# Two-block transformer kernel: order of the last two gate segments, form of the convolution norm, and placement of activation table loads

## What is computed

```python
def hybrid_layer(x, w_in, b_in, conv_w, conv_b, conv_ln_g, conv_ln_b, sinks, w_out, b_out, ln_g, ln_b):
    proj = jnp.einsum("bsd,de->bse", x, w_in) + b_in
    c_val, c_glu, c_gate, q, k, v, a_gate = jnp.split(proj, SPLIT_POINTS, axis=-1)
    y_conv = conformer_conv_branch(c_val, c_glu, conv_w, conv_b, conv_ln_g, conv_ln_b)
    y_conv = y_conv * jax.nn.silu(c_gate)
    y_attn = swa_sink_attention(q, k, v, sinks) * jax.nn.silu(a_gate)
    y = jnp.concatenate([y_conv, y_attn], axis=-1)
    y = jnp.einsum("bse,ed->bsd", y, w_out) + b_out
    return layer_norm(DEEPNORM_ALPHA * x + y, ln_g, ln_b)
```

## Time and profile before

| what | value |
|---|---|
| median of 3 runs (2601.18 to 2603.5) | 2602.79 us |
| the profiled execution's own time | 2602.43 us |
| its span, first to last instruction | 2600.6 us |
| PE busy | 2526.0 us, 97% of the span, 13143 matmuls |
| DVE busy | 1445.0 us, 56% |
| ACT busy | 1208.4 us, 46% |
| mean granted TensorE clock | 0.99 of full speed |

### The profile page before, as it was taken

The page is one execution under the profiler, slowest core; times in us unless marked ns, Lnnn a source line. Parts: engine busy times, 40 slices in busy tenths (PEclk is TensorE's granted clock), DMA queues, the critical chain, the costliest instruction groups (busy, mean ns, idle before and its releaser), DMA issues.

```text
span 2600.6 us, 34916 instructions
## 1 busy us (share of the span) xinstructions
PE 2526.0 (97%) x13143; PEld 2171.3 (83%) x13143; DVE 1445.0 (56%) x1937; ACT 1208.4 (46%) x1569; POOL 46.8 (2%) x58
## 2 busy tenths in 40 slices
PE   8999989999999999999999999999999999999786
PEld 8999978888888888888998888888888888887675
DVE  5555555545545445456755554545454545887755
ACT  5444545444444444445444544444444445556653
POOL 0000000000000000000220000000000001000000
PEclk9999999999999999999999999999999999999988
DMA  7555545666666665555545666666665657664433
GB/s 229 163 170 164 161 153 178 195 192 187 188 190 187 191 191 191 191 188 165 154 137 175 189 187 190 189 187 189 189 192 188 191 190 222 187 179 138 153 108 119
DMA packets 290789, 463.31 MB, mean 178 GB/s; under 512 B 17167, under 2 KB 115649, under 8 KB 290170
## 3 DMA queue, kind: packets, MB, share of 16 engines
q1 hardware_dynamic: 288384, 453.63, 57.6%
q0 software_dynamic: 1680, 8.11, 0.9%
q10 hardware_dynamic: 618, 0.09, 0.0%
HBM read 459.63 MB, written 2.14 MB: 178 GB/s over the span
## 4 chain that ended last, share of the span: by engine, by line
PE 94%; ACT 3%; DVE 2%; issue 1%; ACTq 0%; DVEq 0%
PE PG L246 72%; PE PG L224 12%; PE PG L235 4%; PE PS L767 1%; PE PS L706 1%; ACT ws L196 1%; PE PS L810 1%; PE PS L552 1%; PE PO L830 1%; DVE ws L202 1%; ACT ts L1578 0%; PE PS L768 0%; ACT ts L793 0%; PE PG L1142 0%; PE PO L831 0%
## 5 line engine op out<-in xcount | busy, mean ns | idle before, releaser
L202 DVE TENSOR_TENSOR ws<-raw,ws 128x1024 fp32r<-128x1024 f32 x860 | 1056.0, 1229 | 1059.1 <-ACT ws L196 1054.5
L196 ACT ACTIVATE ws<-raw 128x1024 fp32r<-128x1024 f32 x860 | 911.2, 1060 | 1274.4 <-PE PG L246 1024.1
L246 PE MATMUL PG<-ws,hs 128*128 128x512 f32 x5184 | 1190.6, 390 | 0.0
L246 PEld LDWEIGHTS PG<-ws,hs 128*128 128x128 f32 x5184 | 969.2, 188 | 199.3
L246 PE MATMUL PG<-ws,fs 128*128 128x512 f32 x2112 | 481.3, 389 | 0.0
L246 PEld LDWEIGHTS PG<-ws,fs 128*128 128x128 f32 x2112 | 395.9, 188 | 81.9
L224 PE MATMUL PG<-hs,ws 128*128 128x256 f32 x2640 | 335.6, 287 | 5.9 <-DVEq L1189 3.2
L224 PEld LDWEIGHTS PG<-hs,ws 128*128 128x128 f32 x2640 | 325.1, 194 | 7.7 <-DVEq L1189 3.6
L246 PE MATMUL PG<-ws,os 128*128 128x512 f32 x1152 | 274.6, 399 | 25.2 <-DVE os L1623 10.9
L246 PEld LDWEIGHTS PG<-ws,os 128*128 128x128 f32 x1152 | 219.6, 192 | 72.5 <-issue 19.8
L235 PE MATMUL PG<-ws,hs 128*128 128x256 f32 x864 | 106.6, 284 | 0.0
(11 more groups left out here) (260 smaller groups left out, 868.6 us busy)
## 6 DMA issues: line engine op xcount, KB each, us to landing
raw<-in_w_gate SPq DMA_DIRECT2D x176, 512.0 KB, 4.4
raw<-in_w_up SPq DMA_DIRECT2D x176, 512.0 KB, 3.7
raw<-in_w_down SPq DMA_DIRECT2D x176, 512.0 KB, 3.7
raw<-in_even_w_in SPq DMA_DIRECT2D x96, 512.0 KB, 3.6
raw<-in_w_in SPq DMA_DIRECT2D x52, 512.0 KB, 3.6
raw<-in_odd_w_in SPq DMA_DIRECT2D x44, 512.0 KB, 3.7
raw<-in_even_w_out SPq DMA_DIRECT2D x32, 512.0 KB, 3.6
raw<-in_odd_w_out SPq DMA_DIRECT2D x32, 512.0 KB, 3.8
```

What stands on the lines that cost most here:

```text
L196: e.activation(ws[j % RING][:, :, 0, :], raw[:, j % RING], ACT.Copy).then_inc(s_hi, 1)
L202: e.tensor_tensor(w[:, :, 1, :], raw[:, j % RING], w[:, :, 0, :].bitcast(F32), ALU.subtract).then_inc(s_lo, 1)
L246: ins = e.matmul(out[:, b, :], x_, w[:, kk, :, h, :], start=first and kk == 0 and n == 0, stop=last and kk == 1 and n == 2)
```

## The change

There are six edits. In the diff, the bodies of the removed `mean_pe`, `var_pe`, `mean_dve`, `csq_act`, `tail2_dve`, `tail3_act`, `tail3_dve` and `last_gate` are left out, since they stand in the code above.

1. The segments gAG and gCG change places: the attention gates are projected under slices 0 to 3 and the convolution gates under slices 4 to 7. The silu of the first four attention gate tiles goes to unit 3 of gCG's first group, `att_scale(0)` to its unit 6, `att_hi(0)` and `att_lo(0)` to units 1 and 2 of the second group.
2. The convolution norm is taken about a shift. The mean of tiles 0 to 3 is computed early (`shift_pe`, `shift_dve`, in gAG's first group) and taken off them; `shift_rest` takes it off tiles 4 to 7 at gSO's unit 0. Squares are taken of the shifted values, and one TensorE step (`stats_pe`, at unit 2) gives both the rest of the mean and the mean of squares. The variance is the difference.
3. From there on the tiles go in pairs instead of fours (`conv_scale`, `conv_silu`, `conv_gate`, `conv_hi`, `conv_lo`), spread over units 2, 3 and 4, and TensorE waits for each pair alone.
4. `d_norm` becomes an early hook: ahead of the unit's `hi` and of `rows_out`, where it stood behind `half_out`.
5. The four exponentials of the sinks become one: VectorE adds the sink and the negative maximum (one instruction more in `d_max`), ScalarE takes one exponential of 128x4.
6. A table set that holds both ln and exp (`natural_log_exp_and_others`) is loaded explicitly at the start, in both down projections, ahead of the convolution norm and in gSO's unit 12; the silu's set is loaded explicitly ahead of the convolution's silu.

```diff
+LOG_EXP = "natural_log_exp_and_others"
...
+    gAG = Seg(1, [8, 8], [2, 0])
     gCG = Seg(1, [8, 8], [2, 0])
-    gAG = Seg(1, [8, 8], [2, 0])
...
         table(0, KT, 0, a["attn_norm"][0], "rowsA")
-        w(e, "nat", 1)
-        e.activation(small[:, 0:1], nat[:, 3, P - 1:P], ACT.Copy)
+        e.preload_act_table_set(LOG_EXP)
...
-                 {1: lambda e: turn(e, last)}, {2: lambda e: turn_hi(e, last)}, {3: lambda e: turn_lo(e, last)},
+                 {1: lambda e: turn(e, last)}, {2: lambda e: turn_hi(e, last), 4: lambda e: e.preload_act_table_set(LOG_EXP)},
+                 {3: lambda e: turn_lo(e, last)},
...
+    slots += [(n, g, j, 3 + j % 2) for n in ("Q2", "AG", "CG") for g in (0, 1) for j in range(8)]
...
+        v = sinks[:, 2 * n:2 * n + 2]
+        twice = bass.AP(tensor=v.tensor, offset=v.offset, ap=[list(v.ap[0]), [1, 2], [0, 2]])
+        w(e, "Dnm", n + 1)
+        e.tensor_tensor(es.rearrange("p (h c) -> p h c", c=2), twice, nmx.rearrange("p (h c) -> p h c", c=2), ALU.add).then_inc(sem("Dei"), 1)
...
         exps(e, "D", n)
-        for c in range(4):
-            e.activation(es[:, c:c + 1], sinks[:, 2 * n + c // 2:2 * n + c // 2 + 1], ACT.Exp, bias=nmx[:, c:c + 1]).then_inc(sem("Des"), 1)
+        w(e, "Dei", n + 1)
+        e.activation(es, es, ACT.Exp).then_inc(sem("Des"), 1)
...
+        w(e, "Des", n + 1)
...
+    def shift_pe(e):
+
+        w(e, "cv", 4 * TAP)
+        w(e, "kv", 8)
+        for t in range(4):
+            ins = e.matmul(PO[:, 0, 0:S], ones[:], cacc[:, t, :], start=t == 0, stop=t == 3)
+        ins.then_inc(sem("ck"), 1)
+
+    def shift_dve(e):
+        w(e, "ck", 1)
+        e.tensor_scalar(rn[:], PO[:, 0, 0:S], 1.0 / 512, None, ALU.mult).then_inc(sem("cd"), 1)
+        w(e, "cd", 1)
+        e.tensor_tensor(cacc[:, 0:4], cacc[:, 0:4], bc(rn, 4), ALU.subtract).then_inc(sem("cd"), 1)
+
+    def shift_rest(e):
+        w(e, "cv", 8 * TAP)
+        e.tensor_tensor(cacc[:, 4:8], cacc[:, 4:8], bc(rn, 4), ALU.subtract).then_inc(sem("cd"), 1)
+
     def d_V(e, n):
         w(e, "DpT", n + 1)
+        w(e, "cd", 1)
...
+    def gate_out(e, m, h):
+        t = (8 if m < 8 else 0) + 4 * (m % 2) + 2 * h
+        half_out(e, m, h, POB, gate[:, t:t + 2, :], bin2[:, 26 + t:28 + t] if m < 8 else bin2[:, 16 + t:18 + t])
...
+        seg, g = ((gQ2, 1), (gAG, 0), (gAG, 1), (gCG, 0), (gCG, 1))[m - 5]
...
+    def gate_silu(e, tiles, seen):
+
+        w(e, "gE", seen)
+        e.activation(gate[:, tiles], gate[:, tiles], ACT.Silu).then_inc(sem("gs"), 1)
...
+                if name_of == "AG" and g == 0:
+                    hk[3] = lambda: shift_pe(e)
...
-                    hk[j + 3] = lambda n=n, j=j, half=half: (late_out(e, m0 + g - 1, half), d_norm(e, n), start_at(e, name_of, g, j + 3))
-                if name_of == "AG" and g == 1:
-                    def seven():
-                        late_out(e, m0, 1)
-                        d_norm(e, 7)
-                        w(e, "gE", 18)
-                        e.activation(gate[:, 8:12], gate[:, 8:12], ACT.Silu).then_inc(sem("gs"), 1)
-                        att_hi(e, 0)
-                    hk[7] = seven
+                    hk["early", j + 3] = lambda n=n: d_norm(e, n)
+                    hk[j + 3] = lambda j=j, half=half: (late_out(e, m0 + g - 1, half), start_at(e, name_of, g, j + 3))
+                if name_of == "CG" and g == 0:
+                    hk[3] = lambda: (late_out(e, m0 - 1, 0), gate_silu(e, slice(8, 12), 14), start_at(e, name_of, 0, 3))
+                if name_of == "CG" and g == 1:
+                    hk[1] = lambda: (att_hi(e, 0), start_at(e, name_of, 1, 1))
...
-                if name_of == "AG" and g == 1:
-                    def seven():
-                        d_out(e, 6)
-                        att_scale(e, 0)
-                        taps_at(e, name_of, 1, 7)
-                        att_lo(e, 0)
-                    hk[7] = seven
+                if name_of == "AG" and g == 0:
+                    hk[4] = lambda: (shift_dve(e), taps_at(e, name_of, 0, 4))
+                if name_of == "CG" and g == 0:
+                    hk[6] = lambda: (att_scale(e, 0), taps_at(e, name_of, 0, 6))
+                if name_of == "CG" and g == 1:
+                    hk[2] = lambda: (att_lo(e, 0), taps_at(e, name_of, 1, 2))
...
+    phase(sp=stream(gAG, lambda i, k, j: wide_cols(W2, j, 4352 + 512 * k), wide=1), **gate_run(gAG, "AG", 0, 6))
+    phase(sp=stream(gCG, lambda i, k, j: wide_cols(W2, j, 2048 + 512 * k), wide=1), **gate_run(gCG, "CG", 4, 8))
...
+    def stats_pe(e):
+        w(e, "c2q", 2)
+        w(e, "cd", 3)
         w(e, "DpT", 8)
...
+        for t in range(4, 8):
+            e.matmul(PS[:, 0, 0:S], ones[:], cacc[:, t, :], start=t == 4, stop=t == 7)
         for t in range(8):
             ins = e.matmul(PS[:, 1, 0:S], ones[:], csq[:, t, :], start=t == 0, stop=t == 7)
         ins.then_inc(sem("cm"), 1)
...
+    def csq_act(e, q):
+
+        w(e, "cv", 4 * TAP * (q + 1))
+        w(e, "cd", 2 + q)
+        e.activation(csq[:, 4 * q:4 * q + 4], cacc[:, 4 * q:4 * q + 4], ACT.Square).then_inc(sem("c2q"), 1)
+
+    def spread_dve(e):
+
         w(e, "cm", 1)
...
+        e.tensor_scalar(rn[:], PS[:, 0, 0:S], 1.0 / 1024, None, ALU.mult).then_inc(sem("cd"), 1)
+        w(e, "cd", 4)
+        e.tensor_tensor(na[:], rn[:], rn[:], ALU.mult).then_inc(sem("cd"), 1)
+        w(e, "cd", 5)
+        e.scalar_tensor_tensor(na[:], PS[:, 1, 0:S], 1.0 / 1024, na[:], ALU.mult, ALU.subtract).then_inc(sem("cd"), 1)
+        w(e, "cd", 6)
+        e.tensor_scalar(na[:], na[:], LN_EPS, None, ALU.add).then_inc(sem("LD"), 1)
+        e.tensor_tensor(cacc[:], cacc[:], bc(rn, 8), ALU.subtract).then_inc(sem("cd"), 1)
         rstd_b(e, "L")
...
+    def pair(q):
+        return slice(2 * q, 2 * q + 2)
+
+    def conv_scale(e, q):
+        w(e, "LD", 5)
+        w(e, "cd", 7)
+        e.tensor_tensor(cacc[:, pair(q)], cacc[:, pair(q)], bc(ny, 2), ALU.mult).then_inc(sem("cd"), 1)
+
+    def conv_silu(e, q):
+        w(e, "cm", 1)
+        w(e, "cd", 8 + q)
+        for t in (2 * q, 2 * q + 1):
+            e.activation(csq[:, t, :], cacc[:, t, :], ACT.Silu, scale=clg[:, t:t + 1], bias=clb[:, t:t + 1]).then_inc(sem("cy"), 1)
+
+    def conv_gate(e, q):
         w(e, "gs", 3)
...
+        w(e, "cy", 2 * q + 2)
+        e.tensor_tensor(csq[:, pair(q)], csq[:, pair(q)], gate[:, pair(q)], ALU.mult).then_inc(sem("gm"), 1)
+
+    def conv_hi(e, q):
+        w(e, "gm", 3 + q)
+        e.activation(os_[:, pair(q), 0, :], csq[:, pair(q)], ACT.Copy).then_inc(sem("yh"), 1)
+
+    def conv_lo(e, q):
+        w(e, "yh", 3 + q)
+        e.tensor_tensor(os_[:, pair(q), 1, :], csq[:, pair(q)], os_[:, pair(q), 0, :].bitcast(F32), ALU.subtract).then_inc(sem("y"), 1)
+
+    def third_act(e):
+        att_hi(e, 1)
+        gate_silu(e, slice(0, 8), 20)
+        e.preload_act_table_set(LOG_EXP)
+        rstd_act(e, "L")
+        e.preload_act_table(ACT.Silu)
+        conv_silu(e, 0)
+        conv_silu(e, 1)
+
+    def third_dve(e):
+        att_lo(e, 1)
+        spread_dve(e)
+        conv_scale(e, 0)
+        conv_scale(e, 1)
+
+    so_pe = {0: lambda e: (flips(e, "D", 7), late_turn(e, 9, 0)), 1: lambda e: (d_V(e, 7), late_turn(e, 9, 1)), 2: stats_pe}
+    so_act = {0: lambda e: (flipped(e, "D", 7, turned=False), late_out(e, 9, 0), csq_act(e, 0)),
+              1: lambda e: (gate_silu(e, slice(12, 16), 16), late_out(e, 9, 1), csq_act(e, 1)),
+              2: third_act, 3: lambda e: (conv_silu(e, 2), conv_silu(e, 3), conv_hi(e, 0)),
+              4: lambda e: [conv_hi(e, q) for q in (1, 2, 3)], 12: lambda e: e.preload_act_table_set(LOG_EXP)}
+    so_dve = {0: lambda e: ([tap(e, o) for o in left], shift_rest(e)), 1: lambda e: (d_out(e, 7), att_scale(e, 1)), 2: third_dve,
+              3: lambda e: (conv_scale(e, 2), conv_scale(e, 3), conv_gate(e, 0), conv_gate(e, 1), conv_lo(e, 0)),
+              4: lambda e: (conv_gate(e, 2), conv_gate(e, 3), [conv_lo(e, q) for q in (1, 2, 3)])}
...
+                        w(e, "y", (3, 4, 5, 6, 1, 1, 2, 2)[rows])
```

More of the change, by code:

```diff
@@ L1350, in build @@
     slots += [("K2", 0, j, 2) for j in range(4)]
-    slots += [(n, g, j, 3 + j % 2) for n in ("Q2", "CG", "AG") for g in (0, 1) for j in range(8)]
+    slots += [(n, g, j, 3 + j % 2) for n in ("Q2", "AG", "CG") for g in (0, 1) for j in range(8)]
     plan, begins, op = {}, {}, 0
@@ L1607, in late_out @@
         else:
-            gate_out(e, m, h, **kw)
+            gate_out(e, m, h)
+    def gate_silu(e, tiles, seen):
+        w(e, "gE", seen)
+        e.activation(gate[:, tiles], gate[:, tiles], ACT.Silu).then_inc(sem("gs"), 1)
     def att_scale(e, q):
@@ L1722, in tail3_dve @@
-    def tail3_dve(e):
-        w(e, "gs", 3)
-        for q in range(2):
-            t = slice(4 * q, 4 * q + 4)
-            w(e, "cy", 4 * q + 4)
-            e.tensor_tensor(csq[:, t, :], csq[:, t, :], gate[:, t, :], ALU.mult).then_inc(sem("gm"), 1)
-        for q in range(2):
```

(7 more changed lines are left out.)

49 lines of the change are left out of this document (2 added, 47 removed).

## The result

| | before | after |
|---|---|---|
| median | 2602.93 us (4 runs, 2601.18 to 2603.5) | 2582.44 us (4 runs, 2580.25 to 2583.48) |
| ratio | | 0.9921, 95% interval 0.9904 to 0.9938 |
| profiled execution, its span | 2602.43, 2600.6 us | 2581.7, 2579.9 us |

What follows compares the result with a forecast made beforehand. TensorE, busy 97% of the span, was taken as the bound, so only its waits and lost clock count. Slices 7.0, projection 18.3 and table loads 4.4 sum to 29.7 us: 2602.4 to 2572.7, range 2567 to 2580.

Steps and rivals of the forecast that it cites:

- All 6.96 us should go: Attention slices: TensorE's six later waits for a scaled slice vanish, less some 0.4 us in slice 1; slices gain 7.0 us.
- the stretch up to slice 0: Everything before slice 0's scores, including norms of the first two layers: forecast gain 2.3 us.
- the projection: Output projection with the convolution's end: 121.4 us falls to 103.1, including 1.7 us of lost clock; gain 18.3 us.
- Slower: the scaling ahead of the split: Attention slices, rival: ScalarE and VectorE wait for each other and TensorE starves; a 10 us delay gives 2606 us; chance 0.03.
- The exponentials: Attention slices: four small exponentials of 0.84 us become one, by estimate a quarter of that.
- Slice 0: First attention slice: its 2.3 us wait shrinks by what the shift's matmuls, 1.73 us, fill; gain put at 0.45 us.
- wait ahead of unit 9: Output projection: TensorE waits 1.5 us for unit 9's split, which ends at 38.9 us, behind VectorE's pair steps and gates.
- stops up to 2.3 us without a loss: Ground for the clock estimate: two rows show TensorE stops up to 2.3 us that lose no clock.
- The table loads: Norms: removed loads gain 4.4 us: 2.15 in the last norm, 1.28 in the first layer's, 1.0 in the second's.
- the rival of longer switches: Table switches on ScalarE, rival: each holds it 1.28 us more than its load, time 2570 us; chance 0.03.
- the stop of 2.5 us: Output projection: new TensorE wait near 2.5 us ahead of unit 8, put down to a unit's split, not the convolution tiles.
- a new wait over 3 us: Sign set down for the prediction being wrong: such a wait between units 2 and 9 of the output projection.

Runs made afterwards that it cites:

- norm_back: Changed kernel with only edit 4 undone: the slice's scaling back behind the unit's split and the two bias steps; 2575.84 us, ratio 0.9898.
- combined: Changed kernel with scaling right behind the split, sum ahead of taps, tap starts and first silu behind the probabilities' copy, later shift subtraction, reordered end; 2564.05 us.
- four_exps: norm_back with the four exponentials of the sinks again instead of one, so edits 4 and 5 both undone; 2578.9 us, ratio 0.9912.
- scale_behind_split: Changed kernel with a slice's scaling right behind the unit's split, ahead of the drain and the two bias steps; 2570.03 us, ratio 0.9876.

## Why the prediction was wrong, point by point

- **The step that failed** is in the attention slices: "Behind the scaling now queue the drain and the split, 1.5 us later than before ... so nobody waits for it. All 6.96 us should go". The scaled slice was to have 1.1 us to spare. In the last slice TensorE did turn without a wait, but with nothing to spare: the reciprocal ended at 2457.07, 1.4 us behind the unit instead of the 0.1 taken from the trace before, the scaling at 2458.6, and TensorE turned the slice at 2458.65. Slices 1 and 6 still waited, 1.47 and 1.35 us. And the split was late by the scaling and by the wait for the reciprocal, which comes behind VectorE's taps: 4.7 us behind the unit instead of the 2.6 of norm_back. The cover for it was taken from the wrong reader. TensorE has three units of slack for a split, as the prediction says; VectorE has none, since the split is its next instruction, and its taps, its sum and ScalarE's next tile start hang on it. The stretch lost 4.4 us instead of gaining 7.0, 11.4 us off.
- **How the parts add up.** The other parts made up for some of these 11.4 us: the stretch up to slice 0 gained 4.2 more than forecast, and the projection 1.8 less. Together that is the 9.0 us between the forecast gain of 29.7 and the 20.7 of the two profiles. Of the 4.2, 1.4 are clock near the start that goes with no edit, of which 1.0 was lost again behind the 3.16 us stop of the second layer: luck, not forecast.
- **What is late next** was not asked of the right rows. The forecast took the wait at the turning as free to go to zero; the copy for the scores behind it had 0.38 us to spare behind slice 3 and 0.96 behind slice 1, less than the 1.73 of the stop. combined shows that the gain was there: its slices take 113.1 us, close to the 120.7 - 7.0 = 113.7 forecast, with another order.
- **The rival was named and priced away.** *Slower: the scaling ahead of the split* describes this ring. It got a chance of 0.03, since it looked only for units that come late, and set VectorE's mean load, 12.4 of 15.5 us, against it. A mean doesn't tell where in the slice the reciprocal comes.
- **The exponentials** were put by estimate at a quarter of 0.84 us and took 0.19, which is right. Their length was not priced by itself, and it buys little of TensorE's waits: 0.9 us in all by the trace of four_exps.
- **Slice 0** was right in both terms. From its scores to its turning it took 12.41 us before and 11.96 now, the 0.45 forecast. The shift's matmuls were put at 1.73 us and took 1.54; they filled the first stop.
- **The projection** gained 16.5 of 18.3 us. Waits forecast at 1.0, 1.1, 2.5 and 1.5 were 2.0, 0.75, 2.5 and none; clock was forecast at 1.7 and cost 3.4 (unit 1 took 4.58 us instead of 3.0, the 24 units behind the last stop 67.1 instead of 65.3). The statistics ended 21.2 us behind unit 0, not 18.4, and unit 8 began at 37.8, not 34.6; only the missing wait ahead of unit 9 made up for a part.

```profile
2461.93 4.58 PE L247 MATMUL PG<-ws,os 128*128 128x512 f32 x12
...
2493.44 67.11 PE L247 MATMUL PG<-ws,os 128*128 128x512 f32 x288 [2.49 <-DVE ws L203]
```

- Without the early scaling the projection takes 102.6 us, against 103.1 forecast. The walk itself is near: the statistics end at 19.0, unit 8 begins at 35.6 and unit 9 at 39.7, each within 1 us. That the sum is nearer still is partly luck, since the forecast counts 1.7 us of clock that norm_back's profile didn't lose, and the walk is 1.2 us short. The forecast's ground for small stops, "stops up to 2.3 us without a loss", doesn't hold in the trace before either: behind a stop of 2.27 us near its start 48 matmuls took 7.41 us, and 5.99 in the changed kernel.
- **The table loads**: 7.4 instead of 4.4, mis-sized in the second layer's norm (1.0 forecast, 2.7 measured) and in the first one's clock (0 taken of 0 to 1, 0.9 measured). The last norm gave the 2.1 us forecast. The Trainium skill (ScalarE: Activation LUTs, What ACT_TABLE_LOAD costs) gives about 1283 ns for the load and 1380 ns of drain, 2.66 us for a switch. The trace agrees on the load and not on the drain: in the last norm two loads went and the stretch is 2.1 us shorter, below two bare loads of 1.28, and what follows a load starts 0.01 us behind it. So the rival of longer switches falls.
- Right were the sign, the disappearance of both long stops, the stop of 2.5 us put down to a unit's split, and no load behind the last square. Not as said were the waits at the turning (two over 1 us), the statistics (begun 16.1 us behind unit 0, not 13), the wait ahead of unit 9 (none) and the last matmul (104.9 us, not 101 to 103). Of the signs set down for being wrong, a new wait over 3 us showed, though in the slices and not between units 2 and 9.

## What to carry to other kernels

When a step is moved ahead of a hand-over on an in-order engine, count two delays for whatever now stands behind it: the step's own time and its wait for its input. Then ask each reader of the hand-over for its slack, not only the slowest engine: an engine that reads it as its next instruction has none. A wait that repeats to the hundredth, as the 1.73 and 0.59 us here, points to a series that begins at the waiting engine's own last event; look there first: in norm_back 0.65 us less work ahead of that event shortened no stop, and in scale_behind_split taking work out of the series took the stops away. Before a stop is booked as gain, read how much the next thing had to spare while the stop was there, slice by slice; here it was 0.38 us in the tightest.
